# Two blocks of a transformer on one core: another order in and around the first attention

## The reference

```
cond = silu(c)
mod  = cond @ ada_w[l] + ada_b[l]            # six rows of 1024: shift, scale, gate, twice
h    = x * (1 + sc_m) + sh_m
z    = h @ w_in                              # q, k, v, q_idx, k_idx, w_idx, bg, cg, xb
score = sum over heads of relu(q_idx . k_idx) * w_idx      # 8 index heads of 64
idx   = top_k(score within the chunk limit, 64)
ya    = softmax(q . k[idx] * scale - slope * distance) . v[idx]        # 8 heads of 64
yb    = bg * causal_dwconv(cg * xb, conv_w)                # 512 channels, 3 taps
x     = layer_norm(alpha * x + (1 + g_m) * (concat(ya, yb) @ w_out))
x     = layer_norm(alpha * x + (1 + g_f) * conv_ffn(modulated x))
```

## Time and profile before

| | |
|---|---|
| median of 3 runs | 1253.98 us (1251.09 to 1255.27) |
| the profiled execution | 1247.78 us, span 1245.7 us, mean granted clock 0.965 |
| PE busy | 1155.2 us, 93% of the span |
| DVE, ACT, POOL busy | 559.4, 582.8, 827.4 us |
| stage of the change | about 60 to 188 us of the span |

### The profile page before, as it was taken

How to read it: one execution, slowest core, us unless ns; L and a number is a source line. 1 busy time by engine, 2 the same in 40 slices (tenths; PEclk the granted TensorE clock), 3 DMA queues, 4 the chain that set the end, 5 groups by cost and what they waited for, 6 DMA issues and landing times.

```text
span 1245.7 us, 21662 instructions
## 1 busy us (share of the span) xinstructions
PE 1155.2 (93%) x8119; PEld 1043.1 (84%) x8119; DVE 559.4 (45%) x1149; ACT 582.8 (47%) x868; POOL 827.4 (66%) x290
## 2 busy tenths in 40 slices
PE   6899798999999876999999989999999998999996
PEld 2799687999996873989999959999998987999995
DVE  4359666766557886375322372224211234111113
ACT  0443525554542435354554515455777543554452
POOL 3567448988882730689888825656565765988884
PEclk9899989999998988999999998999999998999998
DMA  9788567999984350678655523444444553666661
GB/s 342 262 292 231 187 209 233 345 335 320 301 301 151 98 136 1 220 227 263 202 179 175 170 65 93 144 135 137 136 139 136 187 165 103 194 192 183 188 185 67
DMA packets 253193, 237.69 MB, mean 191 GB/s; under 512 B 18043, under 2 KB 216496, under 8 KB 253136
## 3 DMA queue, kind: packets, MB, share of 16 engines
q1 hardware_dynamic: 237312, 202.80, 52.6%
q10 hardware_dynamic: 14784, 31.98, 7.1%
q0 software_dynamic: 1040, 2.12, 0.5%
HBM read 235.83 MB, written 1.05 MB: 190 GB/s over the span
## 4 chain that ended last, share of the span: by engine, by line
PE 72%; DVE 8%; ACT 7%; POOL 5%; DMA 5%; issue 2%; SPq 0%; DVEq 0%; POOLq 0%; ACTq 0%
PE bank L1147 18%; PE bank L1148 18%; PE bank L1149 18%; POOL unit_lo L688 5%; ACT unit_hi L790 3%; DMA raw<-in_ev_w_in 2%; PE bank L1186 2%; PE bank L1172 2%; PE bank L1174 2%; PE bank L1218 2%; PE bank L1206 1%; DMA att<-in_ada_w 1%; PE bank L1208 1%; PE bank L1226 1%; PE bank L1327 1%
## 5 line engine op out<-in xcount | busy, mean ns | idle before, releaser
L688 POOL TENSOR_TENSOR unit_lo<-raw,unit_hi 128x2048 fp32r<-128x2048 f32 (+4 forms) x88 | 349.3, 3973 | 261.0 <-ACT unit_hi L790 260.9
L1147 PE MATMUL bank<-h_hi,unit_hi 128*128 128x256 f32 x1248 | 354.2, 284 | 0.3
L1148 PE MATMUL bank<-h_lo,unit_hi 128*128 128x256 f32 x1248 | 353.5, 283 | 0.0
L1149 PE MATMUL bank<-h_hi,unit_lo 128*128 128x256 f32 x1248 | 353.4, 283 | 0.0
L722 POOL TENSOR_TENSOR unit_lo<-raw,unit_hi 128x2048 fp32r<-128x2048 f32 (+1 forms) x70 | 257.2, 3675 | 70.5 <-ACT unit_hi L922 66.9
L1147 PEld LDWEIGHTS bank<-h_hi,unit_hi 128*128 128x128 f32 x1248 | 239.6, 192 | 5.0 <-issue 1.3
L1148 PEld LDWEIGHTS bank<-h_lo,unit_hi 128*128 128x128 f32 x1248 | 239.6, 192 | 2.7
L1149 PEld LDWEIGHTS bank<-h_hi,unit_lo 128*128 128x128 f32 x1248 | 239.6, 192 | 0.0
L790 ACT ACTIVATE unit_hi<-raw 128x2048 fp32r<-128x2048 f32 (+4 forms) x98 | 163.2, 1666 | 105.9 <-PE bank L1149 38.0
L725 POOL TENSOR_TENSOR down<-raw_down,down 128x1024 fp32r<-128x1024 f32 x70 | 176.2, 2517 | 0.0
L1862 DVE SCALAR_TENSOR_TENSOR work<-bank,cols,work 128x254 f32<-128x254 f32 (+1 forms) x176 | 72.7, 474 | 146.9 <-ACT work L909 146.9
(11 more groups left out here) (310 smaller groups left out, 2065.1 us busy)
## 6 DMA issues: line engine op xcount, KB each, us to landing
raw<-in_ffn_w_up SPq DMA_DIRECT2D x88, 512.0 KB, 5.2
raw<-in_w_in SPq DMA_DIRECT2D x60, 512.0 KB, 4.6
raw_down<-in_ffn_w_down SPq DMA_DIRECT2D x44, 512.0 KB, 4.9
raw<-in_w_up SPq DMA_DIRECT2D x64, 256.0 KB, 3.1
raw_down<-in_w_down SPq DMA_DIRECT2D x32, 512.0 KB, 3.5
raw<-in_ev_w_in SPq DMA_DIRECT2D x28, 512.0 KB, 5.3
ada<-in_ada_w ACTq DMA_DIRECT2D x13, 1024.0 KB, 7.8
att<-in_ada_w SPq DMA_DIRECT2D x12, 1024.0 KB, 7.7
```

Of the source, the lines that this page charges most:

```text
L688: nc.gpsimd.tensor_tensor(ul[g % 2][:, w], raw[g % 2][:, w], uh[g % 2][:, w].bitcast(F32), ALU.subtract).then_inc(lo_up, 1)
L1147: nc.tensor.matmul(o, sh, mh, start=first, stop=False)
L1148: nc.tensor.matmul(o, sh, ml, start=False, stop=False)
L1149: return nc.tensor.matmul(o, sl, mh, start=False, stop=last)
```

## The change

Index scores: PE takes QKV0 right behind KI, then the index scores of heads 0 to 3, QKV1, the scores of heads 4 to 7, and QKV2 to QKV5; ACT's relus are in the same order, with QKV0's copy ahead of the first and QKV1's behind the fourth. The search follows the index heads with no modulation half between them; halves 6 and 7 are summed behind it.

Fillers: CX0 to CX3, BG0 and BG1, in twelve half units, are all fillers of the attention. DVE makes the convolutions of CX0, CX2, CX3 in the middle of steps 0 to 2 and that of CX1 at the end of step 0, the gates at the end of steps 2 and 3, and sums halves 8 to 11 at the ends of the four steps. `out_low` and `out_high` stand at other places in this attention, and all its PV products use bank 6 (the sums use 7).

Loads: SP issues the rest of the constants ahead of KI and the gate rows behind it, formerly POOL's. The units go in order of number; half 6 follows QKV1, 7 QKV2, 8 CX0, 9 CX1, 10 CX3, 11 BG1, 12 EO0, 13 EO1.

```diff
--- before.py
+++ after.py
@@ -194,7 +194,7 @@
             turn(("score", a, h), h % 4)
             turn(("tr", a, h), h % 4)
             if h % 2 == 0:
-                turn(("pv", a, h // 2), 6 + h // 2 % 2)
+                turn(("pv", a, h // 2), 6 if a == DSA else 6 + h // 2 % 2)
 
     turn("cond", 6)
     turn("stage", 6)
@@ -470,13 +470,12 @@
             parts = iter([(g, part) for g in units_ for part in range(2)])
             return [[next(parts) for _ in range(n)] for n in counts]
 
-        FILL = {DSA: [[(G_BG[0], 0), (G_BG[0], 1)], [(G_BG[1], 0)], [(G_BG[1], 1)], [], [], [], [], []],
+        FILL = {DSA: halves(G_CX + G_BG, (3, 1, 2, 1, 2, 1, 1, 1)),
                 MLA: [[(None, 0), (None, 1)], [], [], [], [], [], [], []],
                 FOX: halves(G_QKV[MOBA], (3, 1, 2, 1, 2, 1, 1, 1)), MOBA: halves(G_QKVS, (3, 1, 2, 1, 2, 1, 1, 1)),
                 "stick": halves(G_GATE[:10], (3, 2, 3, 2, 3, 2, 3, 2))}
 
         DONE = {a: [[g for g, part in fill if part == 1] for fill in f] for a, f in FILL.items()}
-        DONE[DSA] = [[], [], [G_BG[0]], [], [G_BG[1]], [], [], []]
         DONE[MLA] = [[], [], [0, 1], [], [2], [], [3], []]
 
 
@@ -484,8 +483,8 @@
         MOD_PE = (2, 3)
         MOD_START = 2 * MOD_PE[0]
         SUM_FIRST = [4, 5]
-        SUM_IDX = {0: [6], 2: [7], 4: [8], 6: [9]}
-        SUM_CONV = [10, 11]
+        SUM_TOP = [6, 7]
+        SUM_ATT = [8, 9, 10, 11]
         SUM_EVEN = [12, 13, 14, 15]
         MOD_FFN = 16
         SUM_AFTER = [MOD_FFN + NB_FF, MOD_FFN + NB_FF + 1]
@@ -591,21 +590,17 @@
                 load_unit(g)
             for a in SUM_FIRST:
                 load_ada(a)
-            for g in range(2, G_QKV[DSA][2]):
+            i1 = CONST_AT["ones"][1]
+            sp_.dma_start(cst[:, i1:], consts[:, i1:]).then_inc(const_in, 16)
+            load_unit(G_KI)
+            for w in range(2):
+                load_gates(sp_, 0, w)
+            early = {G_QKV[DSA][1]: SUM_TOP[0], G_QKV[DSA][2]: SUM_TOP[1], G_CX[0]: SUM_ATT[0], G_CX[1]: SUM_ATT[1],
+                     G_CX[3]: SUM_ATT[2], G_BG[1]: SUM_ATT[3], G_EO[0]: SUM_EVEN[0], G_EO[1]: SUM_EVEN[1]}
+            for g in range(G_KI + 1, G_EO[-1] + 1):
                 load_unit(g)
-            for h in range(HEADS):
-                if h % 2 == 0:
-                    load_unit(G_QKV[DSA][2 + h // 2])
-                for a in SUM_IDX.get(h, []):
-                    load_ada(a)
-            for i, g in enumerate(G_CX + G_BG):
-                load_unit(g)
-                if i < 2:
-                    load_ada(SUM_CONV[i])
-            for a in SUM_EVEN[:2]:
-                load_ada(a)
-            for g in G_EO:
-                load_unit(g)
+                if g in early:
+                    load_ada(early[g])
             for a in SUM_EVEN[2:]:
                 load_ada(a)
             for k in range(2):
@@ -736,10 +731,6 @@
                 pool.dma_start(dst, src).then_inc(stage_in, 16)
             lo_unit(0)
             lo_unit(1)
-            i1 = CONST_AT["ones"][1]
-            pool.dma_start(cst[:, i1:], consts[:, i1:]).then_inc(const_in, 16)
-            for w in range(2):
-                load_gates(pool, 0, w)
             for g in range(2, G_EO[-1] + 2):
                 lo_unit(g)
             power(0, mv[:, :, 1], 2, LN_EPS)
@@ -869,9 +860,11 @@
                 for p in range(PAIRS):
                     for h in (2 * p, 2 * p + 1):
                         evac_pt(a, h)
+                    if p and a == DSA:
+                        out_high(a, p - 1)
                     for g in DONE[a][2 * p + 1]:
                         filler(g)
-                    if p:
+                    if p and a != DSA:
                         out_high(a, p - 1)
                     if p + 2 < PAIRS:
                         for h in (2 * p + 4, 2 * p + 5):
@@ -973,23 +966,21 @@
             hi_unit(G_KI + 2)
             b = full(act, "wi")
             nc.scalar.activation(wi, b[:, 0:16], ACT.Copy).then_inc(free("wi"), 1)
+            evac_qkv(G_QKV[DSA][0], 0, 0)
             for h in range(HEADS):
                 b = full(act, ("idx", h))
                 nc.scalar.activation(b[:, 0:384], b[:, 0:384], ACT.Relu).then_inc(idx_relu, 1)
-                if h % 2 == 0:
-                    evac_qkv(G_QKV[DSA][h // 2], 0, h // 2)
-            for j in range(4, 6):
+                if h == 3:
+                    evac_qkv(G_QKV[DSA][1], 0, 1)
+            for j in range(2, 6):
                 evac_qkv(G_QKV[DSA][j], 0, j)
 
-            def cg(i, g):
-                b = unit_full(act, g)
+            def cg(g):
+                i, b = g - G_CX[0], unit_full(act, g)
                 if i >= 2:
                     unit_evacuated(act, g - 2)
                 nc.scalar.activation(cgb[i % 2], b[:, 0:256], ACT.Copy).then_inc(cg_ready, 1)
                 hi_unit(g + 2)
-
-            for i, g in enumerate(G_CX):
-                cg(i, g)
 
             def gated(g):
                 act.wait_ge(bg_ready, g - G_BG[0] + 1)
@@ -998,7 +989,7 @@
                                      ).then_inc(yb_hi, 1)
                 hi_unit(g + 2)
 
-            attention(DSA, gated)
+            attention(DSA, lambda g: cg(g) if g < G_BG[0] else gated(g))
             load_rows(0, W["ln_mix_g"][0:1, :], W["ln_mix_b"][0:1, :])
             for g in G_EO:
                 other(g)
@@ -1432,6 +1423,7 @@
                 unit_cols(g, hh, hl, ready=h_ready(0), high=h_high_ready(0))
 
             unit_cols(G_KI, hh, hl, blocks=(64, 0))
+            unit_cols(G_QKV[DSA][0], hh, hl)
             pe.wait_ge(wi_rows, 1)
             o = begin("wi")
             for tt in range(TT):
@@ -1449,11 +1441,12 @@
                                               start=True, stop=True)
                         if tt == 1:
                             done(mm, ("idx", h))
-                unit_cols(G_QKV[DSA][p], hh, hl)
+                if p == 1:
+                    unit_cols(G_QKV[DSA][1], hh, hl)
+            for g in G_QKV[DSA][2:4]:
+                unit_cols(g, hh, hl)
             for g in G_QKV[DSA][4:6]:
                 unit_rows(g, hh, hl)
-            for g in G_CX:
-                unit_cols(g, hh, hl)
             for g in G_QKV[DSA][2:4]:
                 unit_evacuated(pe, g)
             pe.wait_ge(const_in, 16)
@@ -1803,18 +1796,22 @@
                 V.tensor_tensor(lo[:, p, :], bank[turns["pv", a, p][0]][:, 0:S], hi[:, p, :].bitcast(F32), ALU.subtract
                                 ).then_inc(free(("pv", a, p)), 1)
 
-            def attention(a, between=None):
+            def attention(a, between=None, middle=None):
 
                 for h in range(4):
                     soft(a, h)
                 for h in range(2):
                     normalize(a, h)
                 for p in range(PAIRS):
+                    if p and a == DSA:
+                        out_low(a, p - 1)
                     for h in (2 * p + 2, 2 * p + 3) if p + 1 < PAIRS else ():
                         normalize(a, h)
+                    if middle:
+                        middle(p)
                     for h in (2 * p + 4, 2 * p + 5) if p + 2 < PAIRS else ():
                         soft(a, h)
-                    if p:
+                    if p and a != DSA:
                         out_low(a, p - 1)
                     if between:
                         between(p)
@@ -1986,8 +1983,6 @@
                     else:
                         ins = V.scalar_tensor_tensor(d, t, w, d, ALU.mult, ALU.add)
                 ins.then_inc(free(("idx", h)), 1)
-                for a in SUM_IDX.get(h, []):
-                    modulation_half(a, bank[7][:, :])
             evacuated(dve, ("idx", HEADS - 1))
             dve.wait_ge(const_in, 16)
 
@@ -2001,7 +1996,12 @@
                 link(V.tensor_scalar(m, d, REMOVED / 1.5, BIG, ALU.is_gt, ALU.mult))
                 link(V.tensor_tensor(m, m, C("dist_chunk")[:, P:S] if tt == 0 else C("dist_chunk"), ALU.add))
 
-            for b, g in enumerate(G_CX):
+            for a in SUM_TOP:
+                modulation_half(a, bank[7][:, :])
+
+            def convolution(b):
+
+                g = G_CX[b]
                 o = unit_full(dve, g)
                 dve.wait_ge(cg_ready, b + 1)
                 p_ = o[:, S:2 * S]
@@ -2014,20 +2014,32 @@
                     if back == 1:
                         link(ins)
                 ins.then_inc(unit_free(g), 1)
-                if b < 2:
-                    modulation_half(SUM_CONV[b], bank[7][:, :])
-            unit_evacuated(dve, G_CX[-1])
+
+            def gate(i):
+
+                g = G_BG[i]
+                o = unit_full(dve, g)[:, :].rearrange("p (k t) -> p k t", k=2)
+                for b in (2 * i, 2 * i + 1):
+                    unit_evacuated(dve, G_CX[b])
+                V.tensor_tensor(o, o, ybc[:, 2 * i:2 * i + 2, :], ALU.mult).then_inc(bg_ready, 1)
+                dve.wait_ge(yb_hi, i + 1)
```

(25 more changed lines are left out.)

## The result

| | before | after |
|---|---|---|
| median | 1251.79 us (1248.33 to 1255.27, 5 runs) | 1264.52 us (1259.85 to 1265.39, 5 runs) |
| ratio | | 1.0076, 95% interval 1.0050 to 1.0102 |
| the profiled execution | 1247.78 us, span 1245.7 | 1264.52 us, span 1262.5 |

The medians alone stand 12.7 us apart (1.0102, the upper end of the interval); the ratio is the figure used from here on.

The account below looks back on a forecast made before the run. TensorE bounds the kernel: stalls of 8.7, 1.3, 9.6, 1.3 and 5.6 plus 6.8 of low clock make 33, less 16.9 winnable: 16. Chain's +15.6 gives profiled 1263.4, 1269.6 on the median's scale; point 1269, range 1254 to 1278.

Parts of the forecast that it names:

- EO0 full: Even mixer's EO0 unit done on TensorE at 184.5 us instead of 168.9, +15.6, including 2.8 of low clock.
- EO1 to EO3: Rest of the even mixer follows EO0 without a new wait; nothing behind it gives any of the 15.6 back.
- The lock on the search: Search's six SBUF-only VectorE instructions each wait for a POOL operation in flight: end 101.0 us, unhindered 95.1.
- the sums themselves: Modulation sums in the four softmax steps, 12.4 us on VectorE, cost nothing on PE but through SP.
- Low clock, 1.0 + 3.0 + 2.8: TensorE time lost to lowered clock: 1.0 by CX1's second half, 3.0 behind the second pause, 2.8 in EO0.
- EO2's load, 8.1 us behind half 13: EO2's load, issued after half 11's sum at about 173.5, lands at 181.6, its low part ready when PE asks.
- The first addition of the search: VectorE's first search addition loses 1.1 us to POOL's low part; comparisons lose 1.6 and 3.3.
- The rest of the span: Behind the even mixer nothing gives any back, since FFN's first units hang on EO2's low part as before.
- The scale of the median: Profiled execution 1247.78 stands 6.2 us under the median 1253.98, so forecast 1263.4 becomes 1269.6.
- A: Rival, attention: filler covers, SP's waits cost nothing and 16.9 us go, to 1237; chance 0.12.
- B: Rival, lighter: lock spares the search (95.1), landings take 7.1, clock holds: +2.4, 1256, up to 1262; chance 0.20.
- C: Rival, heavier: search to 102.8 (+1.8), landings of 9.95 (+5.5): 1277; chance 0.08.

Follow-up runs that it names:

- both: Changed kernel with modulation halves loaded behind the units that had waited with them, and the search in PSUM bank 7: 1243.4 us, 0.9936 of the kernel before.
- the changed kernel again: The changed kernel, unaltered, timed a second time against the kernel before: ratio 1.0096 (1.0069 to 1.0123).
- the best version: Changed kernel with halves behind units, search in PSUM, first FFN load ahead of half 15's, ACT's BG0 and EO1 high parts later: 1236.5 us, 0.9875 of the kernel before.

## Why the prediction was right, and where it was off

| step | forecast | measured |
|---|---|---|
| search starts | 79.4 | 79.8 |
| search ends | 101.0 | 101.0 |
| CX1 landed | 112.2 | 113.0 |
| CX1's second half done | 124.5 | 124.3 |
| half 8 summed, BG0 landed | 133.5, 141.6 | 133.2, 141.6 |
| second pair's `weighted` | 145.2 | 145.2 |
| half 10 summed, EO1 landed | 166.8, 174.9 | 165.1, 173.1 |
| EO0 full | 184.5 (+15.6) | 181.7 (+12.7, VectorE's wait for it) |
| EO1 to EO3 | no new wait | norm at +14.4 |
| profiled execution | 1263.4 | 1264.5 |

**Right, and shown.** The mechanism: a half ahead of a unit in SP's queue makes the unit wait for the sum two halves earlier. Half 8 and half 10 moved back each took away the pause that the forecast had named for it (9.1 to the 3.9 + 0.7 that the search leaves, 9.7 to 0.3), half 12 brought EO0's from 4.6 to 1.1, and all of them together turned +9.5 to +12 us into -3.8. The lock on the search was there: with PSUM under it the comparisons take 0.30 and 0.43 instead of 1.62 and 3.50.

**Right, and argued.** That the sums themselves cost TensorE nothing except through SP: in the kernel **both** TensorE waits 3.8 us in all from 99 to 151 us (1.8, 1.4 and twice 0.3), while VectorE makes the four sums of halves 8 to 11. No run took the sums out of there.

**Terms that were mis-sized.**
- *Low clock, 1.0 + 3.0 + 2.8.* The rows give, as time in which TensorE worked below full speed times the share lost: behind the second pause 2.8 x 0.50 + 4 x 0.11 = 1.9 instead of 3.0; in EO0 4 x 0.43 = 1.7 instead of 2.8. I had taken the 3.4 us of the earlier trace rows, where two pauses in a row kept it low. The first 1.1 are most of the 1.7 us by which half 10's sum came earlier than forecast, and that 1.7 and the last 1.1 make the 2.8 us at EO0. The size scatters: in the changed kernel again the same reckoning gives 4.2, 2.3 and 2.1 us behind the three pauses, against 1.3, 1.9 and 1.7 here.
- *EO2's load, 8.1 us behind half 13.* It took 12.1, and EO2 waited 1.4; the sum had said that nothing waits from there. It had not counted ACT's norm rows, two loads that go out beside it and are the likely reason (not tested). The 1.4 make up most of the step from +12.7 at EO0 to +14.4 at the norm; the two errors partly cancelled.
- *The first addition of the search* lost 0.8 instead of 1.1, the comparisons 1.3 and 3.1 instead of 1.6 and 3.3; the late start of 0.4 and some 0.3 more in the rest of the search made up for it.
- *The rest of the span*, +2.4 us behind the norm. Over all the kernels' traces this remainder lies between -4.3 (the changed kernel again: norm +16.8, span +12.5) and +2.7, with the same code behind the norm, so it is scatter. The profiled figure was therefore hit partly by luck.
- *The scale of the median.* I added the 6.2 us by which the profiled execution stood under the median of the runs shown. The new profiled execution stands exactly on its median, and the kernel before is at 1251.8 over more runs. On ratios of many runs the change costs 9.5 to 12 us, not 15.6: one execution's trace is some 3 us uncertain each way, and the trace of the kernel before, 4.0 us under its median, is a quick one. The sum of +15.6 met the +14.4 between two traces; over many runs the change costs a quarter to a third less, so part of the agreement on size is luck.

**The rivals.** A (the filler covers) is what the change becomes with its loads in order: it named 1237, and the best version ran at 1236.5, though for a part by the search in PSUM and the FFN load's new place, which A did not contain; loads in order alone gave 1247. B's lighter lock fell: the search ended at 101.0. C's slow landing of 9.95 appeared only at EO2, and there as 12.1.

## To carry to other kernels

In an in-order queue a load may wait for nothing later than what its own buffer needs: before a sum is moved back in the program, look at which loads stand behind the load that waits for it. A filler is worth only what its data's arrival allows; here twelve half units stood ready on paper, while the raw data of CX1 and BG0 were issued behind a sum. When one bound is taken away, look at the next in the same queue: the order of two loads, some 70 us behind the search, was worth as much as the search's lock (5.8 and 4.2 us by the ratios, 3.8 and 4.7 at the norm).

## What the runs showed of the hardware

- A VectorE addition of 8 columns, both inputs in SBUF, took 3.63 us beside a POOL low part, 0.16 without one. By the Trainium skill, SBUF — State Buffer, section "Who interferes with whom", a VectorE instruction with two SBUF inputs and a GpSimd one that reads SBUF exclude each other for a whole instruction; the traces agree, down to the smallest one. In the changed kernel `MAX8` and `MATCH_REPLACE8` kept 0.43 and 0.41 us beside POOL's low part from 89.39 to 94.02, as long as later without one: these were not delayed.

```profile
90.14 0.43 DVE L1993 MAX8 small<-work 128x8 f32<-128x256 f32 x1
...
90.68 0.41 DVE L1994 MATCH_REPLACE8 work<-small,work 128x256 f32<-128x256 f32 x1
```

- A VectorE addition whose output lies in PSUM but whose two inputs lie in SBUF was delayed all the same (1.12 and 1.02 us). The one at 87.12, with one input in PSUM and its output in SBUF, took 0.29 beside the low part from 83.55 to 88.18. So what frees an instruction here is an input in PSUM, not its output.
- The same kernel's clock comes back at different moments behind the same pause: pair 0 stood at 124.3 and 126.0 us in two executions of the changed kernel.
